# Retention V projected in one go of 512 columns, and attention units sooner, group by group and wider apart, in a block with two hybrid layers

## The reference

```
# block
xn = rms_norm(x, mix_norm);  proj = xn @ w_in + b_in           # 1024 -> 4352 columns
q(512) k(128) v(128) cb cc cx(512 each) ga gc(1024 each) = split(proj)
attn  = sliding_window_attention(q, k, v, sinks)   # 8 heads of 64, 2 kv groups, window 128, sink in the softmax
conv  = cb * causal_depthwise_conv(cc * cx)        # 3 taps
h     = x + (sigmoid(ga) * (attn @ w_attn_branch) + sigmoid(gc) * (conv @ w_conv_branch)) @ w_out
h     = h + (silu(gate) * val) @ w_down            # gate, val = conv of rms_norm(h) @ w_up, 2 x 2816 columns
# two hybrid layers
aq ak av ag rq rk rv rg = split(rms_norm(x) @ w_in_2)           # eight times 512 columns
ya = chunked attention, 8 heads of 64, relative bias, over chunks of 64 with 8 chunks to the left
yr = rms_norm(chunkwise retention), 4 heads of 128, rotary q and k, decay per head
x  = x + [ya * silu(ag), yr * silu(rg)] @ w_out_2
```

## Time and profile before

| what | value |
|---|---|
| time, median of 3 runs | 1186.59 us (1185.8 to 1186.91) |
| the profiled execution's own time | 1185.57 us |
| span of its profile | 1183.8 us |
| busy: TensorE / its weight loads | 1172.0 / 983.4 us |
| busy: VectorE / ScalarE / GpSimd | 896.3 / 577.1 / 246.5 us |
| granted clock of TensorE, mean | 0.998 |
| moved by DMA | 146.81 MB, 124 GB/s |

### The profile page before, as it was taken

How to read it: one execution, slowest core, us unless ns; L and a number is a source line. 1 busy time by engine, 2 the same in 40 slices (tenths; PEclk the granted TensorE clock), 3 DMA queues, 4 the chain that set the end, 5 groups by cost and what they waited for, 6 DMA issues and landing times.

```text
span 1183.8 us, 14982 instructions
## 1 busy us (share of the span) xinstructions
PE 1172.0 (99%) x5539; PEld 983.4 (83%) x5539; DVE 896.3 (76%) x1482; ACT 577.1 (49%) x972; POOL 246.5 (21%) x223
## 2 busy tenths in 40 slices
PE   9999999999999999999999999999999999999997
PEld 7887788888888888888888888899888888898886
DVE  6889855656776487546776788997897878998876
ACT  6677623324343243325444477764335577753432
POOL 0220399931100000000003602101502311112200
PEclk9999999999999999999999999999999999999999
DMA  6455533333331533233332347663223376663521
GB/s 197 128 170 170 158 90 102 94 98 98 125 94 54 155 90 101 78 111 103 89 107 76 120 134 224 195 175 92 72 72 107 107 205 178 190 185 116 143 89 72
DMA packets 216717, 146.81 MB, mean 124 GB/s; under 512 B 6250, under 2 KB 205380, under 8 KB 216516
## 3 DMA queue, kind: packets, MB, share of 16 engines
q1 hardware_dynamic: 216628, 145.86, 42.3%
q10 hardware_dynamic: 16, 0.00, 0.0%
HBM read 127.49 MB, written 18.35 MB: 123 GB/s over the span
## 4 chain that ended last, share of the span: by engine, by line
PE 87%; DVE 7%; ACT 3%; issue 2%; DMA 1%; POOL 0%; DVEq 0%; SPq 0%; ACTq 0%
PE ps L191 86%; ACT a_p L161 1%; DVE tmp L164 1%; DVE wlo L164 1%; DVE a_p L178 1%; DVE a_pd L182 1%; DVE x1h L167 1%; DVE a_zc L167 0%; ACT whi L161 0%; DMA raw<-in_w_in_dram 0%; DMA xtm<-in_x_dram 0%; DVE smx L164 0%; ACT x1h L161 0%; PE ps L194 0%; DVE a_pt L164 0%
## 5 line engine op out<-in xcount | busy, mean ns | idle before, releaser
L161 ACT ACTIVATE whi<-raw 128x1024 fp32r<-128x1024 f32 (+2 forms) x199 | 206.9, 1045 | 293.5 <-PE ps L191 282.4
L164 DVE TENSOR_TENSOR wlo<-raw,whi 128x1024 fp32r<-128x1024 f32 (+2 forms) x193 | 252.1, 1311 | 43.7 <-ACT whi L161 43.2
L191 PE MATMUL ps<-x0h,whi 128*128 128x512 f32 x1008 | 254.8, 391 | 1.2 <-ACT whi L161 1.2
L191 PE MATMUL ps<-x0h,wlo 128*128 128x512 f32 x1008 | 254.4, 391 | 0.0
L191 PE MATMUL ps<-x0l,whi 128*128 128x512 f32 x1008 | 254.1, 390 | 0.0
L191 PEld LDWEIGHTS ps<-x0h,whi 128*128 128x128 f32 x1008 | 187.4, 188 | 39.6 <-ACT whi L161 1.5
L191 PEld LDWEIGHTS ps<-x0l,whi 128*128 128x128 f32 x1008 | 188.0, 188 | 38.8 <-DVE x0l L167 0.2
L191 PEld LDWEIGHTS ps<-x0h,wlo 128*128 128x128 f32 x1008 | 187.9, 188 | 38.4
L164 POOL TENSOR_TENSOR sums<-sums,sq 128x512 f32<-128x512 f32 x28 | 43.0, 1549 | 446.2 <-ACT sq L161 446.2
L191 PE MATMUL ps<-x1h,wlo 128*128 128x512 f32 x304 | 82.1, 389 | 0.0
L191 PE MATMUL ps<-x1l,whi 128*128 128x512 f32 x304 | 82.1, 389 | 0.0
(11 more groups left out here) (213 smaller groups left out, 1636.4 us busy)
## 6 DMA issues: line engine op xcount, KB each, us to landing
raw<-in_w_in_dram SPq DMA_DIRECT2D x98, 512.0 KB, 4.1
raw<-in_w_up_dram SPq DMA_DIRECT2D x44, 512.0 KB, 3.8
raw<-in_w_out_dram SPq DMA_DIRECT2D x24, 512.0 KB, 3.6
turned<-b_pd SPq DMA_DIRECT2D x16, 640.0 KB, 3.5
raw<-in_w_down_dram SPq DMA_DIRECT2D x16, 512.0 KB, 3.7
b_px<-turned SPq DMA_DIRECT2D x32, 160.0 KB, 3.4
b_p<-turned SPq DMA_DIRECT2D x32, 160.0 KB, 3.6
turned_a<-a_pd SPq DMA_DIRECT2D x6, 512.0 KB, 2.6
```

The lines of the kernel that those rows point to most:

```text
L161: return AC.put(lambda e: e.activation(o, i, func, **kw), after, AC, 1)
L164: return on.put(lambda e: e.tensor_tensor(o, a, b, op), after, on, 1)
L191: return PE.put(lambda e: e.matmul(o, l, r, start=start, stop=stop), after, PE if mark else None, 1)
```

## The change

1. Of the 12 tiles of the conv branch, GpSimd makes the low half of tiles 12, 14, 15 and 17 of the plan; before of 6, 8, 9, 11, 12 and 14. VectorE makes the others.
2. At the start the high half of feature tile k = 1 is made by VectorE, and the low half of k = 0 comes after it.
3. V of the block is transposed in bank 5, not in bank 3.
4. The units of the sliding attention go group by group and not block by block, are put in from the end of q's projection j = 1, one projection sooner, and stand 4.5 steps apart on the mean, not 4; the bank of AV goes by n alone.
5. Both pairs of retention heads get V by one call of 512 columns, in four banks (5, the next two, 6), where before the first of two calls of 256 stood. `project_v(j0)` now serves both uses. The retention heads stand at 68, 76, 84 and 90; counted against the list of projections the second V call before the third head's K is gone.
6. Of the last output tile the half that ScalarE scales is sent by a DMA on ScalarE's queue.

```
             for n, m in enumerate((14 + j, 10 + j, 6 + j)):
-                plan_fm(win, m, on_pool=j < 3 and n != 1)
+                plan_fm(win, m, on_pool=j > 1 and n != 1)
...
-            order += [20, 16, "v", 21, 17, "v", 22, 18, 23, 19, 28, 29, 30, 31]
+            order += [20, 16, "vr", 21, 17, 22, 18, 23, 19, 28, 29, 30, 31]
...
-            X0.th[k] = act(hi, PS[bank][:, :], scale=MIX(k), after=[tp, t_mix])
-            X0.tl[k] = stt(lo, PS[bank][:, :], MIX(k), f32(hi), ALU.mult, ALU.subtract, after=[tp, X0.th[k]])
+            if k == 1:
+                X0.th[k] = ts(hi, PS[bank][:, :], MIX(k), None, ALU.mult, after=[tp, t_mix])
+            else:
+                X0.th[k] = act(hi, PS[bank][:, :], scale=MIX(k), after=[tp, t_mix])
...
-            free = claim(3)
+            free = claim(5)
...
-            u = (2 * n + g) % 2
+            u = n % 2
...
-            if j == 2:
-                for i, (n, g) in enumerate((n, g) for n in range(4) for g in range(2)):
-                    later(3 + 4 * i, unit_a(g, n))
+            if j == 1:
+                for i in range(8):
+                    later(3 + (9 * i + 1) // 2, unit_a(i // 4, i % 4))
...
+            def project_v(j0):
+
+                n = 64 if j0 == 0 else 128
+                ws = [W.take() for _ in range(4)]
+                bs = [7, 5, banks.next(), banks.next()] if j0 == 0 else [5, banks.next(), banks.next(), 6]
                 r, tr_ = st["r"]
 
                 def evac(bank, t, tok):
 
-                    src = PS[bank][:, :].rearrange("p (j h c) -> p j h c", j=2, c=64)
-                    to = [v_at(j, t).rearrange("p s (e c) -> p (s e) c", c=128) for j in range(2)]
+                    free = [(), ()] if j0 == 0 else [[v_read[0], v_read[1]], [q_read[2], q_read[3]]]
+                    src = PS[bank][:, :].rearrange("p (j h c) -> p j h c", j=2, c=n)
+                    to = [v_at(j0 + j, t) for j in range(2)]
...
-                evs += [[2], [3], [], [ev_g(4), ev_g(5), ev_g(6), ev_g(7)]][s - 4]
-            for i, n in enumerate((66, 74, 82, 88)):
+                evs += [[2], [], [], [ev_g(4), ev_g(5), ev_g(6), ev_g(7)]][s - 4]
+            for i, n in enumerate((68, 76, 84, 90)):
                 at_step(n - 1, a_step_later(ret(i)))
...
-                t_done = dma(out[0][128 * t:128 * t + 128, 0:512], ob[:, t, 0:512], d_out, after=tf)
+                t_done = dma(out[0][128 * t:128 * t + 128, 0:512], ob[:, t, 0:512], d_out, after=tf, on=AC)
```

More of the change, by code:

```diff
@@ L472, in block_then_hybrid_layers @@
             order = [4, 0, 5, 1, "va", 12, 6, 2, 13, 7, 3, 14, 15]
-            order += [20, 16, "v", 21, 17, "v", 22, 18, 23, 19, 28, 29, 30, 31]
-            v_cols = iter([3072, 3328])
+            order += [20, 16, "vr", 21, 17, 22, 18, 23, 19, 28, 29, 30, 31]
             for m in order:
-                if m == "va":
+                if m in ("va", "vr"):
                     for k0 in range(0, 8, 2):
[L478 to L482, removed]
+                        plan_tm(wi2, k0, 1024 if m == "va" else 3072, 2, 512)
                 else:
@@ L567, in x_features, with low @@
             hi, lo = X0.hi[:, k, :], X0.lo[:, k, :]
-            X0.th[k] = act(hi, PS[bank][:, :], scale=MIX(k), after=[tp, t_mix])
-            X0.tl[k] = stt(lo, PS[bank][:, :], MIX(k), f32(hi), ALU.mult, ALU.subtract, after=[tp, X0.th[k]])
+            if k == 1:
+                X0.th[k] = ts(hi, PS[bank][:, :], MIX(k), None, ALU.mult, after=[tp, t_mix])
+            else:
+                X0.th[k] = act(hi, PS[bank][:, :], scale=MIX(k), after=[tp, t_mix])
+            def low():
+                X0.tl[k] = stt(lo, PS[bank][:, :], MIX(k), f32(hi), ALU.mult, ALU.subtract, after=[tp, X0.th[k]])
+            if k:
+                if k == 1:
+                    lows.pop()()
+                low()
+            else:
+                lows.append(low)
             def rest():
@@ L574, in x_features @@
             return tp, rest
-        rests = {}
+        rests, lows = {}, []
         for c in range(4):
@@ L716, in evac_v @@
             yield 1
-            src = PS[3][:, :].rearrange("p (b g d) -> p g b d", b=4, g=2)
+            src = PS[5][:, :].rearrange("p (b g d) -> p g b d", b=4, g=2)
             for g in range(2):
@@ L723, in evac_v @@
             vv_tok.extend([th, tl])
-            bank_free[3] = [th, tl]
+            bank_free[5] = [th, tl]
         def evac_q(j):
@@ L1188, in ev_q @@
                 return go
[L1190 to L1234, removed]
@@ L1236, in project_va @@
-            def project_va():
-                ws, bs = [W.take() for _ in range(4)], [7, 5, banks.next(), banks.next()]
+            def project_v(j0):
+                n = 64 if j0 == 0 else 128
+                ws = [W.take() for _ in range(4)]
+                bs = [7, 5, banks.next(), banks.next()] if j0 == 0 else [5, banks.next(), banks.next(), 6]
                 r, tr_ = st["r"]
                 def evac(bank, t, tok):
-                    src = PS[bank][:, :].rearrange("p (j h c) -> p j h c", j=2, c=64)
-                    to = [v_at(j, t).rearrange("p s (e c) -> p (s e) c", c=128) for j in range(2)]
+                    free = [(), ()] if j0 == 0 else [[v_read[0], v_read[1]], [q_read[2], q_read[3]]]
+                    src = PS[bank][:, :].rearrange("p (j h c) -> p j h c", j=2, c=n)
+                    to = [v_at(j0 + j, t) for j in range(2)]
+                    if j0 == 0:
+                        to = [v.rearrange("p s (e c) -> p (s e) c", c=128) for v in to]
@@ L1245, in evac @@
                     for j in range(2):
-                        th = act(to[j][:, :, 0:64], src[:, j], scale=r[:, t:t + 1], after=[tok, tr_])
+                        th = act(to[j][:, :, 0:n], src[:, j], scale=r[:, t:t + 1], after=[tok, tr_, free[j]])
                     yield 1
                     for j in range(2):
-                        tl = stt(to[j][:, :, 64:128], src[:, j], r[:, t:t + 1], f32(to[j][:, :, 0:64]), ALU.mult, ALU.subtract,
-                                 after=[tok, tr_, th])
+                        tl = stt(to[j][:, :, n:2 * n], src[:, j], r[:, t:t + 1], f32(to[j][:, :, 0:n]), ALU.mult, ALU.subtract,
+                                 after=[tok, tr_, th, free[j]])
@@ L1251, in evac @@
                     bank_free[bank] = [th, tl]
                     for j in range(2):
-                        tok_v.setdefault(j, []).extend([th, tl])
+                        tok_v.setdefault(j0 + j, []).extend([th, tl])
                 for kb in range(4):
```

8 lines of the change are left out of this document (3 added, 5 removed).

## The result

The change made the kernel slower: 1197.95 us (1196.19 to 1200.28, five runs) against 1185.8, a ratio of 1.0098 [1.0084, 1.0112], where 1183.2 had been forecast. The profiled execution took 1196.87 us, span 1195.0.

What follows compares the result with a forecast made beforehand. TensorE's end-to-end list of matmuls was taken as the bound (busy 1172.0 of 1183.8 us). Terms -2.5 + 3.5 - 3.9 - 0.4 - 0.1 = -3.4 us gave a median of 1183.2 us, range 1180.1 to 1187.2.

Steps and rivals of the forecast that it cites:

- Retention V: Both hybrid layers: 192 matmuls of 512 columns replace 384 of 256, all saved on TensorE's path, -2.5 us.
- two new waits could eat this: Retention V: waits for bank 6 (margin 0.4 us) and the second head's scores; 0 taken, at most 0.6 and 1 per layer.
- First unit, +3.5: First attention unit's QK^T: stall for VectorE's q0 and q1 low halves, done at 44.2 not 40.7, +3.5 us (2.4 to 4.6).
- Rival (c): Behind the new first-unit stall the granted clock falls to 1.2 GHz for one or two steps: +1.8 to +3.6 us; chance 0.10.
- The three AV waits, -3.9: Sliding attention: AV products' three stalls for a_pt go because VectorE catches up, -3.9 us (bounds -3.9 and 0).
- the gift: First-unit stall: VectorE works on while TensorE stands, so its lateness falls by 3.5 us at once.
- the slow rival: Units 3 to 6: VectorE stays late, fed by GpSimd splits meeting a_pt's; +3.4 us, 1190.0; chance 0.07.
- Tail, -0.4: Last output transfers: two DMA issues go together on two queues, -0.4 us (bounds 0 and -0.4).
- Start, -0.1: Kernel start: TensorE's 1.2 us wait for ScalarE's first weights shrinks, -0.1 us taken (bounds 0 and -1.2).
- Rival (d): AV of units 3 to 6: VectorE stays late, four AV products wait 1.7 us each; +3.4 us, 1190.0; chance 0.07.

Runs made afterwards that it cites:

- e1: The changed kernel with the output products of both hybrid layers in banks 1, 2, 6, 0 instead of 0, 1, 2, 6: 1191.78 us, ratio 1.0045.
- e4: The kernel before with edit 5 alone (retention V in one call of 512 columns, heads at 68, 76, 84, 90): 1191.03 us, ratio 1.0041.
- e6: Edits 5 and 6 alone on the kernel before, with two more draws from the bank rotation after the second V call: 1192.29 us, ratio 1.0054.
- e11: The whole change with output products in banks 1, 2, 4, 6 (first hybrid layer) and 1, 2, 6, 4 (second): 1190.33 us, ratio 1.0027.
- e10: Edits 5 and 6 alone on the kernel before, output products in banks 1, 2, 4, 6 and 1, 2, 6, 4: 1185.27 us, ratio 0.9990.
- e5: The changed kernel with 14 matmuls of 512 columns, product unread, in front of the second layer's output product: 1195.62 us.
- e8: The changed kernel with the GpSimd splits of the kernel before (tiles 6, 8, 9, 11, 12, 14): 1195.84 us, ratio 1.0076.
- e15: The kernel of e11 with all attention units one step later: 1184.54 us, ratio 0.9986.
- e17: The kernel of e16 with the GpSimd splits of the kernel before: 1180.23 us, ratio 0.9953.
- e12: The kernel of e10 with attention units one step later from the fourth on, two from the fifth: 1183.49 us, ratio 0.9972.
- e16: The kernel of e15 with the first attention unit yet one step later: 1181.44 us, ratio 0.9965.
- e13: The kernel of e10 with the attention units group by group at the old steps: 1185.81 us.

## Why the prediction was wrong, step by step

*Retention V, "all of it lies on the path: -2.5", and "two new waits could eat this".* The larger of two steps that failed. I looked for waits at the edit's own places (bank 6, the second retention head; neither waits, as forecast) and put the outputs at nothing: not what the edit does to the rotation behind it, nor how late VectorE is there. Shown by e1, e4, e6 and e11: 2.2 and 2.7 us of wait and the clock behind the second, 7.6 us in all. That the reuse of the bank makes these waits is shown, since other banks take them away; why VectorE comes to it 3 us later than before isn't. The saving itself was right: 2.4 us from start to start, in the change as in e4 and e10.

*First unit, +3.5.* Right in place, cause and size: the eight matmuls were done at 44.19 and not at 40.7, 3.5 us, of which the view calls 3.0 idle.

*Rival (c), the granted clock, chance 0.10.* It came true, 1.7 us behind the first unit and 2.8 behind the second output. That idleness brings it is shown by e5. The Trainium skill, "TensorE: Matmul & The Clock Gate", Part 1, has the clock fall to half rate after idleness; the trace agrees, with 0.51 behind the 2.74 us. The length of a gap alone doesn't decide it: the waits of 2.06 at 127.67 and 2.16 at 883 left the clock at 1.00 in this execution, one of 2.15 at the first layer's output brought it to 0.72 for 6 us in e8's, and in e10's it fell behind gaps of 1.5 us and less, the very gaps that cost nothing in the trace of before. I gave it too little because I had that one trace. Times and mean clocks of the kernel before in other runs (beside e1: 1185.4 us at 1.000, 1187.6 at 0.997) fit with a fall in some of its executions too.

*The three AV waits, -3.9, because the first wait lets VectorE catch up.* The second step that failed: 3.6 against 3.3 us idle, 4.3 against 3.9 from start to start, so 4.3 us of the miss. e15 to e17 speak against the reasoning itself, since the AV waits fall as the first wait goes. VectorE did catch up, and no further:

```profile
51.51 0.69 DVE L167 SCALAR_TENSOR_TENSOR tmp<-ps,rb 128x512 f32<-128x512 f32 x1 [2.00 <-PE ps L191]
```

At 51.51 it had idled 2.00 us for TensorE's product, so the rest of the gift was never spent, and by 105 it was late again (the first AV wait of the change stands at 105.49). Why the units are late at just the changed steps isn't settled. VectorE waits much for ScalarE's a_p, with nothing else to do in its list; its waits from 41 to 146 us, of the change and of e12:

```profile
DVE a_pd L182 <- ACT a_p L161: 7.8, 6, 1.8
```
```profile
DVE a_pd L182 <- ACT a_p L161: 6.8, 6, 1.8
```

It is 4.1 before, and 4.6, 3.8 and 2.6 in e15, e16 and e17, falling as the AV waits fall; but e12 has 6.8 with only 2.7 us of AV waits, so it is not the cause alone. And GpSimd holds VectorE: two a_xml halves took 3.13 us while a split ran from 96.59, which the prediction named as the slow rival's food. It is a part: 0.6 us of AV waits by e8, 1.0 by e17, with the units where these runs have them.

*Tail, -0.4.* The issues go side by side as said, the transfers land later by about as much: 0. *Start, -0.1*: the first product comes 0.45 sooner, and the first QK^T at 39.74 as before: 0.

*Rival (d), slower by the AV of units 3 to 6*, had the sign and not the mechanism. The sum now: +5.3 in the attention (3.5 first wait, 1.7 clock, 0.4 AV, and -0.3 in small steps not traced), +1.3 and +4.6 at the outputs (2.4 and 3.0 of wait from start to start, 2.8 of clock behind the second, less 1.2 of V in each layer), 11.2 together. The forecast had -3.4. Of the 14.6 us between them 8.2 lie at the outputs, 4.3 at the AV products, 1.7 in the clock behind the first unit and 0.5 at the tail and the start.

## What to carry to other kernels

An edit that takes fewer turns from a rotation moves every later user of it: compare, on the list of instructions, which buffer the next stage opens with, who held it last, and how late the engine is that has to empty it. On an engine that is busy 99% a gap of two or three microseconds can cost as much again in clock (2.8 us behind 2.74 here), so a stage that starts sooner than its operands can be worse than one that starts a step late, as e11 and e15 were by 5.8 us. And test the edits of a change apart: here, with the banks and the first steps put right and the splits left as they were, the rest came to 0.9953 [0.9940, 0.9967] of the time before.

## What was not expected of the hardware

The changed kernel ran 4.1 us apart from run to run, and 0.6 us apart once the waits at its outputs were gone (e11). Such scatter needs no gap of that length: the runs of the kernel before, beside e10, and of e13 lay 5.0 and 5.5 us apart, and their traces have no wait over 1.7 us. Two queues for the last two output transfers gave nothing: 2.5 and 2.7 us to landing side by side, 2.2 one behind the other.
